# First expert's rows gathered already turned, block by block between its gate slots; the once-loaded slot is the 12th

## What is computed

```python
def expert_choice_ffn(h, w_router, w_gate, w_up, w_down):
    aff = jax.nn.softmax(jnp.einsum('bsd,de->bse', h, w_router), axis=-1)
    g, idx = lax.top_k(aff.transpose(0, 2, 1), cap)          # cap = 64
    xe = h[bidx, idx]
    hid = (jax.nn.silu(jnp.einsum('becd,edf->becf', xe, w_gate))
           * jnp.einsum('becd,edf->becf', xe, w_up))
    ye = jnp.einsum('becf,efd->becd', hid, w_down) * g[..., None]
    return jnp.zeros_like(h).at[bidx, idx].add(ye)
# x = x + expert_choice_ffn(rms_norm_2(x, norm_ffn_g), ...); return rms_norm_2(x, norm_f_g)
```

## Time and profile before

| | us |
|---|---|
| median of 3 runs | 1969.47 |
| the runs | 1969.24 to 1972.62 |
| profiled execution, its own time | 1970.42 |
| its span | 1968.6 |
| busy: PE / PEld / DVE / ACT / POOL | 1884.6 / 1146.5 / 729.1 / 516.8 / 58.6 |
| mean granted clock | 0.989 |

### The profile page before, as it was taken

One profiled execution on the slowest core, in us unless ns is written; L12 is line 12 of the kernel. 1 busy time (PEld: TensorE's weight loads), 2 busy tenths in 40 slices (PEclk: granted clock), 3 DMA queues, 4 the chain that ended last, 5 costly groups with the idle time before them and its releaser, 6 DMA issues.

```text
span 1968.6 us, 20653 instructions
## 1 busy us (share of the span) xinstructions
PE 1884.6 (96%) x8719; PEld 1146.5 (58%) x8719; DVE 729.1 (37%) x1216; ACT 516.8 (26%) x836; POOL 58.6 (3%) x58
## 2 busy tenths in 40 slices
PE   8999999999999999999997999999889998999898
PEld 6788888888887888877874333333333332333332
DVE  7544444333356765886453111111111110111112
ACT  5444323222245343276622000000000000000002
POOL 1000000000014001000010000000000000000000
PEclk9999999999999999999998999999999999999999
DMA  5221322322323234212387999999999999999997
GB/s 190 86 86 65 118 96 97 97 97 96 107 95 107 75 112 161 75 65 78 141 328 292 430 432 434 430 432 433 433 432 434 430 433 433 431 433 433 431 429 294
DMA packets 50476, 506.89 MB, mean 257 GB/s; under 512 B 6544, under 2 KB 7568, under 8 KB 31696
## 3 DMA queue, kind: packets, MB, share of 16 engines
q1 hardware_dynamic: 48288, 502.22, 62.3%
q10 hardware_dynamic: 2096, 3.35, 0.5%
HBM read 501.23 MB, written 4.33 MB: 257 GB/s over the span
## 4 chain that ended last, share of the span: by engine, by line
PE 73%; DMA 23%; DVE 2%; ACT 2%; issue 1%; ACTq 0%; SPq 0%; DVEq 0%
PE ps L2133 40%; DMA ring_a<-in_experts_in 23%; PE ps L2484 10%; PE ps L2495 7%; PE ps L2068 4%; PE ps L2443 2%; PE ps L2467 1%; PE ps L2305 1%; PE ps L2530 1%; PE ps L2282 1%; PE ps L2506 0%; ACT hidT L1255 0%; PE ps L2183 0%; PE ps L2180 0%; PE ps L2186 0%
## 5 line engine op out<-in xcount | busy, mean ns | idle before, releaser
L2484 PE MATMUL ps<-ring_a,xe 128*64 128x512 f32 x1504 | 343.8, 610 | 41.9 <-DMA ring_a<-in_experts_in 41.1
L2484 PEld LDWEIGHTS ps<-ring_a,xe 128*64 128x64 f32 x1504 | 107.0, 140 | 272.8 <-issue 211.4
L1300 DVE TENSOR_TENSOR d_lo<-d_raw,d_hi 128x1024 fp32r<-128x1024 f32 x166 | 204.4, 1240 | 118.9 <-ACT d_hi L850 118.2
L2133 PE MATMUL ps<-n_hi,d_hi 128*128 128x512 f32 x448 | 176.0, 393 | 1.5 <-DVE d_lo L1300 0.8
L2133 PE MATMUL ps<-n_lo,d_hi 128*128 128x512 f32 x448 | 174.5, 389 | 0.0
L2133 PE MATMUL ps<-n_hi,d_lo 128*128 128x512 f32 x448 | 174.3, 389 | 0.0
L850 ACT ACTIVATE d_hi<-d_raw 128x1024 fp32r<-128x1024 f32 x166 | 170.8, 1049 | 8.6 <-DMA d_raw<-in_tiles_in 6.9
L1530 DVE TENSOR_TENSOR hid<-hid,ps 128x512 f32<-128x512 f32 x32 | 20.7, 684 | 409.1 <-PE ps L2484 382.7
L1976 DVE TENSOR_TENSOR acc<-acc,ps 128x1024 f32<-128x1024 f32 x56 | 64.6, 1215 | 244.5 <-PE ps L2467 244.5
L2495 PE MATMUL ps<-ring_a,hidT 128*64 128x512 f32 x648 | 145.9, 596 | 8.7 <-DMA ring_a<-in_experts_in 5.5
L2484 PE MATMUL ps<-ring_b,xe 128*64 128x512 f32 x464 | 103.1, 593 | 1.6 <-DMA ring_b<-in_experts_in 1.6
(11 more groups left out here) (499 smaller groups left out, 2710.6 us busy)
## 6 DMA issues: line engine op xcount, KB each, us to landing
ring_a<-in_experts_in SPq DMA_DIRECT2D x56, 4096.0 KB, 41.8
ring_b<-in_experts_in SPq DMA_DIRECT2D x28, 3072.0 KB, 42.7
d_raw<-in_tiles_in SPq DMA_DIRECT2D x166, 512.0 KB, 3.3
ring_a<-in_experts_in SPq DMA_DIRECT2D x31, 1024.0 KB, 12.4
ring_a<-in_experts_in SPq DMA_DIRECT2D x12, 2048.0 KB, 13.4
ring_b<-in_experts_in SPq DMA_DIRECT2D x5, 2048.0 KB, 13.2
ring_b<-in_experts_in SPq DMA_DIRECT2D x8, 1024.0 KB, 16.6
x_in<-in_xT_in SPq DMA_DIRECT2D x4, 512.0 KB, 6.7
```

Of the source, the lines that this page charges most:

```text
L1300: dve.tensor_tensor(d_lo[:, n % SLOTS, :, :], d_raw[:, n % SLOTS, :, :], d_hi[:, n % SLOTS, :, :].bitcast(F32), ALU.subtract).then_inc(t_l ...
L2133: mm = pe.matmul(bank, lt[:, n, gr.k0 + k, :], rt[:, k, :], start=k == 0 and m == 0, stop=k == gr.nk - 1 and m == 2)
L2484: mm = pe.matmul(ps[half * CAP:(half + 1) * CAP, 2 * m + q, :], xe[:, k, :], slot(e, n)[:, (2 * q + half) * S:(2 * q + half + 1) * S], sta ...
```

## The change

The first expert's x2 rows are no longer gathered as rows and then turned. `gather_first(k)` takes a block of 128 features of x2 as weights and `picks` as the moving side (64 columns), four matmuls summed over the four groups of tokens; the result is block k of the turned rows. It lies in bank 4 + k % 4. VectorE multiplies block by block by the gain into `xe[:, k]`. TensorE does blocks 0 and 1, then gate slot 0, block 2, gate slot 1, and so on to block 7, gate slot 6, gate slot 7; each gate slot waits for its block of xe, blocks 4 to 7 for the bank of the block four before. The copy, the transposes and `xg_first` go. The once-loaded slot is number 11 (the fourth up slot) in place of 3; the counts that the refills wait for are 1, 2, 3, 4, 5, 6 (single), then 8, 10, 13, 15 and on as before. Silu and `pickg` of the first expert wait for slot 11. The counters are set up anew; only what touches the order is shown:

```diff
-ONCE = 3
+ONCE = 11
@@ ScalarE
-            gathered(0)
             for e in range(NE - 1):
-                used(act, e, 7)
+                used(act, e, 7 if e else ONCE)
@@ VectorE
+            def entered_first():
+                for k in range(KD):
+                    dve.wait_ge(first_pe.sem, first_pe.count(f"rows{k}"))
+                    first_dve.done(mul(xe[:, k, :], ps[:, 4 + k % 4, 0:CAP], vcol("ffn", k).to_broadcast([P, CAP])), f"xe{k}")
...
             choose(0)
-            entered(0)
+            entered_first()
...
                 if e + 1 < NE:
-                    dve.wait_ge(x_pe.sem, x_pe.count("gather", e))
+                    if e:
+                        dve.wait_ge(x_pe.sem, x_pe.count("gather", e - 1))
+                    else:
+                        dve.wait_ge(first_pe.sem, first_pe.count(f"rows{KD - 1}"))
                     dve.wait_ge(e_dve.sem, e_dve.count("pg1", e))
                     choose(e + 1)
@@ TensorE
+            def gather_first(k):
+                if k >= 4:
+                    pe.wait_ge(first_dve.sem, first_dve.count(f"xe{k - 4}"))
+                for t in range(TT):
+                    if k == 0:
+                        pe.wait_ge(first_dve.sem, first_dve.count(f"picks{t}"))
+                    mm = pe.matmul(ps[:, 4 + k % 4, 0:CAP], x2[:, t, k * P:(k + 1) * P], picks[:, t, :], start=t == 0, stop=t == TT - 1)
+                first_pe.done(mm, f"rows{k}")
...
-            gather(0)
-            gather_turned(0)
+            gather_first(0)
             for e in range(NE - 1):
-                pe.wait_ge(x_dve.sem, x_dve.count("xe" if e else "xea", e))
-                gate_up(e, 0)
-                if e:
+                if e == 0:
+                    for k in range(KD):
+                        if k + 1 < KD:
+                            gather_first(k + 1)
+                        pe.wait_ge(first_dve.sem, first_dve.count(f"xe{k}"))
+                        gate_up(0, k)
+                    for n in range(KD, 2 * KD):
+                        gate_up(0, n)
+                else:
+                    pe.wait_ge(x_dve.sem, x_dve.count("xe", e - 1))
+                    gate_up(e, 0)
                     placed(e - 1)
...
```

More of the change, by code:

```diff
@@ L442, in kernel_program @@
         xg = at("xg", [P, S], 199.5)
-        xg_first = at("xg_first", [P, S], 194.5)
         once = at("once", [P, FF], 197.5)
@@ L614, in kernel_program @@
         s_used = sem("ring_used")
-        x_pe = Steps(sem("gather_pe"), ["gather", "xgTa", "xgT"], 16)
-        x_act = Steps(sem("gather_act"), ["xga", "xg"], 16)
-        x_dve = Steps(sem("gather_dve"), [f"picks{t}" for t in range(TT)] + ["pick", "xea", "xe"], 16)
+        first_pe = Steps(sem("gather_pe"), [f"rows{k}" for k in range(KD)])
+        first_dve = Steps(sem("gather_dve"), [f"picks{t}" for t in range(TT)] + ["pick"] + [f"xe{k}" for k in range(KD)])
+        x_pe = Steps(first_pe, ["gather", "xgTa", "xgT"], 15)
+        x_act = Steps(sem("gather_act"), ["xga", "xg"], 15)
+        x_dve = Steps(first_dve, [f"picks{t}" for t in range(TT)] + ["pick", "xea", "xe"], 15)
         e_pe = Steps(sem("expert_pe"), ["hT", "place", "o0", "o1", "o2", "o3"], 15)
@@ L666, in slot @@
             return slots(e * PER + n, 1)
-        def turned_bank(e, n):
-            return 5 if e else 6 + n
         def tiles4(ap):
@@ L1243, in gathered @@
             def gathered(e):
-                act.wait_ge(x_pe.sem, x_pe.count("gather", e))
+                act.wait_ge(x_pe.sem, x_pe.count("gather", e - 1))
                 for c, name in ((0, "xga"), (256, "xg")):
-                    x_act.done(act.activation((xg if e else xg_first)[:, c:c + 256], ps[:, 5, c:c + 256], ACT.Copy), name)
-            gathered(0)
+                    x_act.done(act.activation(xg[:, c:c + 256], ps[:, 5, c:c + 256], ACT.Copy), name)
             for e in range(NE - 1):
-                used(act, e, 7)
+                used(act, e, 7 if e else ONCE)
                 for q in range(2):
@@ L1956, in choose @@
             def choose(e):
+                steps = x_dve if e else first_dve
                 at = pos[:, :, e:e + 1].to_broadcast([P, TT, CAP])
@@ L1959, in choose @@
                 for t in range(TT):
-                    x_dve.done(dve.tensor_scalar(picks[:, t, :], iot[:, :], pos[:, t, e:e + 1], esm[:, 8 + t:9 + t],
+                    steps.done(dve.tensor_scalar(picks[:, t, :], iot[:, :], pos[:, t, e:e + 1], esm[:, 8 + t:9 + t],
                                                  ALU.is_equal, ALU.mult), f"picks{t}")
-                x_dve.done(dve.tensor_tensor(pick[:, :, :], at, number, ALU.is_equal), "pick")
-                dve.wait_ge(x_dve.sem, x_dve.count("pick", e))
+                steps.done(dve.tensor_tensor(pick[:, :, :], at, number, ALU.is_equal), "pick")
+                dve.wait_ge(steps.sem, steps.count("pick", e - 1 if e else 0))
+            def entered_first():
+                for k in range(KD):
+                    dve.wait_ge(first_pe.sem, first_pe.count(f"rows{k}"))
+                    first_dve.done(mul(xe[:, k, :], ps[:, 4 + k % 4, 0:CAP], vcol("ffn", k).to_broadcast([P, CAP])), f"xe{k}")
             def entered(e):
                 for n, name in enumerate(("xea", "xe")):
-                    dve.wait_ge(x_pe.sem, x_pe.count("xgT", e))
+                    dve.wait_ge(x_pe.sem, x_pe.count("xgT", e - 1))
                     x_dve.done(dve.tensor_tensor(xe[:, :, :].rearrange("p (h c) s -> p c h s", h=2)[:, 2 * n:2 * n + 2],
-                                                 ps[:, turned_bank(e, n), :].rearrange("p (c h s) -> p c h s", c=4, h=2)[:, 2 * n:2 * n + 2],
+                                                 ps[:, 5, :].rearrange("p (c h s) -> p c h s", c=4, h=2)[:, 2 * n:2 * n + 2],
                                                  gain[:, 2 * n:2 * n + 2], ALU.mult), name)
@@ L2440, in gather @@
                 for t in range(TT):
-                    pe.wait_ge(x_dve.sem, x_dve.count(f"picks{t}", e))
+                    pe.wait_ge(x_dve.sem, x_dve.count(f"picks{t}", e - 1))
                     for d in range(2):
@@ L2449, in gather_turned @@
                     if c % 2 == 0:
-                        pe.wait_ge(x_act.sem, x_act.count("xg" if e or c else "xga", e))
-                    mm = pe.transpose(ps[:, turned_bank(e, c // 2), c * P:(c + 1) * P], (xg if e else xg_first)[:, c * P:(c + 1) * P], ident[:, :])
+                        pe.wait_ge(x_act.sem, x_act.count("xg", e - 1))
+                    mm = pe.transpose(ps[:, 5, c * P:(c + 1) * P], xg[:, c * P:(c + 1) * P], ident[:, :])
                     if c % 2:
@@ L2534, in residual @@
                 pe.matmul(ps[:, bank, :], ident[:, :], acc[:, t, d * S:(d + 1) * S], start=True, stop=False, skip_group_check=True)
-            gather(0)
-            gather_turned(0)
+            gather_first(0)
             for e in range(NE - 1):
-                pe.wait_ge(x_dve.sem, x_dve.count("xe" if e else "xea", e))
-                gate_up(e, 0)
-                if e:
-                    placed(e - 1)
[L2543 to L2547, removed]
+                if e == 0:
[9 more added lines that the diff above has]
+                    gate_up(e, 0)
+                    placed(e - 1)
+                    for n in range(1, KD):
+                        gate_up(e, n)
                     pe.wait_ge(e_dve.sem, e_dve.count("o2", e - 1))
-                for n in range(KD, 2 * KD):
-                    gate_up(e, n)
-                if e:
+                    for n in range(KD, 2 * KD):
+                        gate_up(e, n)
                     pe.wait_ge(e_dve.sem, e_dve.count("o1", e - 1))
@@ L2561, in _ @@
                     if i == 6:
-                        pe.wait_ge(x_dve.sem, x_dve.count("xe", e + 1))
+                        pe.wait_ge(x_dve.sem, x_dve.count("xe", e))
                         e_pe.done(place_turned(e), "place")
@@ L2566, in _ @@
             e = NE - 1
-            pe.wait_ge(x_dve.sem, x_dve.count("xe", e))
+            pe.wait_ge(x_dve.sem, x_dve.count("xe", e - 1))
             gate_up(e, 0)
```

## The result

The changed kernel takes 1974.42 us (median of 13 runs, 1973.91 to 1975.70), the kernel before 1970.59 on the same chip (13 runs, 1969.01 to 1972.62). The ratio is 1.0019 with a 95% interval of 1.0012 to 1.0027, so +3.7 us (the two medians are 3.8 apart). The profiled execution took 1974.30 against 1970.42, +3.9.

The account below looks back on a forecast made before the run. Bound: the weight stream, tied to TensorE up to the 27th slot. Gate and up end 3.2 us later despite a 3.5 us earlier first refill, so the stream ends +2.9: 1969.47 + 2.9 = 1972.4 us, range 1968.0 to 1975.5.

Parts of the forecast that it names:

- rival 2: TensorE's clock rises later under the 64-column blocks, losing 1.7 us of work: +4.6, 1974.1 us; chance 0.21.
- The bound: The weight stream sets the end; it is tied to TensorE's progress up to the 27th slot and free later.
- The 0.35 us of the earlier trace: Small dip of 352 and 360 GB/s from 1127 to 1129, after the issue for 27 used slots at 1125.93.
- the last place in which the stream is short: The pair waiting for 27 used slots; after it TensorE takes 51 us for what takes the stream 58.
- First slot free, first refill 3.5 us earlier: Gate slot 0 free at 1067.5 against 1071.0, so the first refill starts 3.5 us earlier.
- The blocks: Eight TensorE blocks of 64-column matmuls: 0.92 us each at full clock, 1.71 at half, plus 0.2 for switching weights.
- Rival 4: Blocks are cheap, 64 instructions near 25 ns; gate and up end 3.5 us earlier: 1966.0 us; with rival 3 0.11.
- The clock: TensorE's clock stays at 0.50 until about 1066.1, covering 1.0 us of gate slot 0; the rest takes 1.22.
- The sum: TensorE's first matmul at 1061.69, last gate and up slot done at 1099.95, 3.2 us later than 1096.74.
- the 0.6 that I left to the pair: Up to 0.6 us the pair for 27 slots could spare, so the stream ends 2.6 to 3.2 later.
- Rival 3 (the early start decides): Stream not held at the 27th slot, so earlier first refill moves the end: up to -3.5, 1966.0; with rival 4 0.11.
- The covers: Expert 0's silu and pickg, waiting for slot 12, finish before gather(1) near 1100; uncovered they would cost some 2 us.

Follow-up runs that it names:

- once_alone: Kernel before with only the once-loaded slot moved from number 3 to 11: 1970.38 us, ratio 1.0001.
- delay_first: Kernel before plus five unread 512-column matmuls in the first expert, ahead of the gather for the second: 1973.72 us, ratio 1.0019.
- delay_fourth: Kernel before plus five unread 512-column matmuls in the fourth expert: 1970.47 us, ratio 1.0000.
- delay_second: Kernel before plus five unread 512-column matmuls in the second expert, ahead of the gather for the third: 1972.58 us, ratio 1.0009.
- after_warm2: Changed kernel plus ten unread matmuls, eight during the search for the 64 largest and two in the gaps after it: 1970.61 us, ratio 0.9998 to kernel before.
- blocks_once3: Changed kernel with the once-loaded slot back at number 3, so the blocks alone: 1974.66 us, ratio 1.0021 to the kernel before.
- after_single: Changed kernel with the refills of slots 31 to 52 one by one instead of in pairs: 1973.24 us, ratio 1.0018 to the kernel before.
- after_warm: Changed kernel plus eight unread matmuls while VectorE looks for the 64 largest: 1972.62 us, ratio 1.0012 to the kernel before.
- before_single: Kernel before with the refills of slots 31 to 52 one by one instead of in pairs: 1969.36 us, ratio 0.9998.
- before_warm: Kernel before plus eight unread matmuls while VectorE looks for the 64 largest: 1967.25 us, ratio 0.9988.
- before_warm2: Kernel before plus ten unread matmuls, eight during the search for the 64 largest and two in the gaps after it: 1967.77 us, ratio 0.9984.
- before_best: Kernel before plus ten unread matmuls, refills of slots 31 to 52 one by one, and once-loaded slot number 11: 1965.46 us, ratio 0.9975.

## Why the prediction came out as it did

**The number.** The forecast was 1972.4, the measured median is 1974.42, 2.0 above. Of this 1.1 is the kernel before itself, whose median is 1970.59 in 13 runs and was 1969.47 in the three runs that the forecast started from; 0.9 is the change, +3.8 in place of +2.9. The result lies nearer to rival 2 (1974.1) than to the forecast.

**The bound: right.** The end is the end of the stream, tied to TensorE in the second expert and free later. once_alone, delay_first and delay_fourth show it. The 0.35 us of the earlier trace rows that led there was a weaker sign than I took it for. The DMA share is 1.00 and 0.96 in these two windows, and over seven us around them only 0.2 us are missing. Too narrow was "the last place in which the stream is short": that is so for the kernel before, but a delay of 4.6 us behind the 40th slot still cost 1.8 (delay_second), for the spare time at the following refills is small. For the changed kernel that makes no difference; its delay is there at the 27th slot already.

**First slot free, first refill 3.5 us earlier: mechanism right, size off.** It was 3.0, with a start that was 0.75 earlier in itself. The reason is the clock, below. Two sums were off in themselves. By its own terms the pair for 8 used slots comes at 1067.5 + 6.72 + 7 x 1.715 = 1086.2, not 1085.3; measured is 1087.61. And gate and up end before the change at 1096.98 by the chain in the earlier trace rows, not at 1096.74.

**The blocks: right.** I took 0.92 us for a block and 0.2 for the switch of weights, 1.12. Measured are 1.03 in the block and 1.87 in place of 1.715 in the slot behind it, 1.19 together. The row of 32 columns was a good bound for 64: at clock 1.00 an instruction with 128-column weights took 0.115 us with 32 moving columns and 0.123 to 0.13 with 64. At 0.50 the blocks took 3.65 / 16 = 0.228. Rival 4 (25 ns an instruction, by the Trainium skill's page "TensorE: Matmul & The Clock Gate", section "Back-to-back issue gap") falls with the 0.123 of after_warm2. By the Trainium skill's page "TensorE: Matmul & The Clock Gate", section "LDWEIGHTS (loading the stationary operand)", a load takes its columns over 1.2 GHz, an estimated 107 ns for 128. The trace comes near this at clock 1.00 (0.115 to 0.13) and not at 0.50 (0.228).

**The clock: the step that failed.** I let it rise at 1066.1 as before, with 1.0 us of gate slot 0 ahead of it. It rose at 1068.7, and gate slot 0 took 3.61 us where I had 1.0 + 1.22 and 0.2 for the switch. That was my rival 2, to which I gave 0.21, and in the trace that is the case that came. From the first matmul of the gather it took 7.7 us in the changed kernel, in blocks_once3, after_single and after_warm about 7.9, 6.1 and 6.8; under the 512-column gather 4.4 in the kernel before, and 2.7 to 4.9 in the five runs that have its gather and no extra matmuls ahead. Part of this spread is when the clock had fallen. From that fall (at 1053.6 to 1056.8, while TensorE was idle) to the rise it stayed at 0.50, read from windows of 0.25 us, for 10.2 us in all six runs with the old gather and no extra matmuls, and for 13.7 us in all three with blocks and none. So it isn't the chance of one execution, and the 3.4 us longer are those that rival 2 named. Only the way the rows are gathered differs there; what in the blocks keeps the clock low no run separates. The path from the first matmul to the last up slot says the same: 39.6 to 40.4 us in the four changed kernels with a low clock, 34.5 to 35.5 in the six others, 4.9 apart in the mean; 3.6 apart at 1.00 throughout. About 1.3 us of the longer path is the clock.

**The sum.** From the first matmul to the last up slot I had 38.3 us and the trace has 40.4. The 2.1 us between them are 0.2 in the two blocks at 0.50 (3.65 for 3.42), 1.5 in gate slot 0 and the block behind it (3.61 + 1.27 for 2.42 + 0.92), where the clock was late, and 0.3 in the other slots and blocks. I had TensorE 3.2 us late and the stream 2.9. TensorE's path was 5.1 longer; less the earlier start, the issue was 4.33 late; the time rose by 3.7 (3.9 in the profile). Of the 0.6 that I left to the pair, 0.4 was there. The forecast of +2.9 was short by the clock's term, which the earlier start of that execution partly made good. That offset is luck and was no term of the sum: "first matmul at 1061.69 as before" was wrong by 0.75 us, since the clock did not fall around 1046 in that execution.

**Rival 3 (the early start decides): wrong.** The stream started 3 us earlier and this was lost by the end of the pause from 1087 to 1090, as the sum had it: slots free every 2.90 us (forecast 2.84) against 2.43 for 1 MB. **The covers held:** silu and pickg behind slot 12 cost nothing that can be measured (once_alone).

## What to carry to other kernels

Where one engine feeds frees to a long transfer stream, an earlier first free is worth nothing if the engine is later at the tightest free: tabulate for each transfer how long it is issued before the data ahead of it end, and look at the smallest of these before cutting the start. Work that is split into narrow matmuls to overlap a copy costs its weight loads, here 64 loads against 20 with the transposes, and cost more here where it stood in the stretch in which the clock had yet to rise. Idle time of TensorE ahead of a critical stretch can be filled with matmuls that nobody reads: here worth 2.4 to 3.2 us in the kernel before.

## What the runs showed of the hardware

- With TensorE busy all the time, the clock rose from 0.50 to 1.00 6.1 to 7.9 us after the first matmul of the 64-column blocks and 2.7 to 4.9 us after that of the 512-column gather. The stretch at 0.50 lasted 13.7 us in the three profiled executions with blocks and 10.2 in the six without, extra matmuls left aside.
- An issue into a stream that still runs needs some 1.5 us of lead, by my estimate from these rows: the pair for 27 slots in the kernel before went out 1.1 us ahead of the first window that is short (1127) and 0.2 to 0.35 us was lost; the refill for 42 slots had some 4.6 us and nothing was lost.
- Whether the clock falls around 1046 differs from execution to execution of the same code and is worth 1.0 us. From the first of the 24 matmuls of 32 columns to the first matmul of the gather it is 18.8 us where the clock fell (the kernel before, once_alone, delay_first, delay_fourth, before_single, blocks_once3) and 17.8 where it did not (the changed kernel, after_single, delay_second); with the extra matmuls 18.1 (before_warm, before_warm2, before_best) and 17.1 (after_warm, after_warm2). So it fell in eight of nine executions with the old gather and in one of five with blocks. What stays open is whether that is chance, and with it how much of the earlier start stands in the 13 runs behind each median.
